# A fused two-block model on one core: narrower outputs in one mixer, a woven order in another

## The chip, the core and the metric

One core of a Trainium2 chip runs one program. The time is that of one launch on the device, in microseconds (us); the median of three runs is compared. TensorE (PE) multiplies, VectorE (DVE) and ScalarE (ACT) do elementwise work, GpSimd (POOL) and SyncE (SP) issue most DMAs here.

## What is computed

Two transformer blocks in a row on 256 tokens of width 1024, all in f32, two layers each. Block one puts 16 meta tokens ahead of the input and drops them at the end:

```python
for l in range(DEPTH):
    h = h + 0.5 * rmsnorm(swiglu(rmsnorm(h, g_pre_ffn1[l]), w_ffn1_gu[l], w_ffn1_down[l]), g_post_ffn1[l])
    mix = token_mixer(rmsnorm(h, g_pre_mix[l]), ...)      # causal softmax attention (fox) + gated linear attention (gla)
    h = h + rmsnorm(mix, g_post_mix[l])
    h = h + 0.5 * rmsnorm(swiglu(rmsnorm(h, g_pre_ffn2[l]), w_ffn2_gu[l], w_ffn2_down[l]), g_post_ffn2[l])
return h[:, BLOCK:]                                       # the 256 tokens
# in token_mixer
o_gla = from_heads(o_gla) * jax.nn.silu(gr)
y = jax.nn.sigmoid(g_merge_a) * (from_heads(o_fox) @ w_fox_o) + jax.nn.sigmoid(g_merge_b) * (o_gla @ w_gla_o)
return y @ w_out
```

Block two has a mLSTM mixer in its first layer and a dilated attention mixer in its second, which is the last mixer of the program:

```python
p = h @ w_q
q_d = rms_norm(p[..., :DIL_WIDTH]..., q_gain)             # 12 heads in 3 groups, 4 memory heads
# per group: s = q k^T * scale + bias(bucket of distance), masked, softmax, weighted by the groups' denominators
h_m = memory_cross_attention(p[..., DIL_WIDTH:], mem_n, w_mem_kv, mq_gain, mk_gain)   # 256 memory tokens, 4 heads
return jnp.concatenate([h_d, h_m], axis=-1) @ w_out
```

## The kernel before

One program holds a list of instructions for each engine, written out by hand, in an order that `weave` (L215) makes: a main generator yields once a step, and after each step every side generator goes on by one. Side work starts where it compares `c.step` with a number. Engines are tied by semaphores only.

**Weights.** All weights come as 723 slabs of up to 512 KB (128 partitions x 1024 f32) in the order in which `weights` (L140) lists them, through a ring of `RING = 7` slots (L26). SyncE issues slab u when `used` says that u − 7 is done (L430). ScalarE rounds a slab to fp32r (`whi`, L1243), VectorE takes the rest (`wlo`, L1906), both some `LEAD = 4` slabs ahead, and TensorE makes three products of eight matmuls each, high·high, high·low, low·high (`products`, L518). Activations are in such pairs too (`xhi`, `xlo`), with tokens as columns: 272 (`cols1`: 16 meta tokens and 256) or 256 (`cols2`).

**Order.** For each of two layers: ffn, `mixer1`, ffn. Then ffn 4, `mixer2a`, ffn 5, `shared_kv`, ffn 6, `mixer2b`, ffn 7. Each ffn has 22 steps j with a gate and an up slab, then 22 down slabs.

**`mixer1(L)`** (TensorE L711, ScalarE L1402, VectorE L2119). All projections have 272 columns in both layers. Softmax attention is done in 24 units a layer (`fox_units`, L415): 4 pairs of heads, query tiles of 128, 128 and 16 tokens, 2 heads, with 1, 2 and 3 key tiles. They are a side generator from step `FOX_AT = 13`, three deep: scores of unit i, turns of unit i − 2, values of unit i − 3. After the last step come the products with `w_fox_o` and `w_gla_o` (`fo`, `go`, L843), each half slab four k deep, gating on VectorE (L2357), and `wo`, which in the second layer already has 256 columns.

**`mixer2b`** (TensorE L1107, ScalarE L1812, VectorE L2652). (1) Four query slabs, the statistics matmul (`stat`), then the table of position biases: VectorE makes a 33x128 operand per head (`bias_table`, L2644), TensorE multiplies it with the one-hot table `ohb` (33x512), so that all 128 rows are equal, ScalarE copies it and sends 256 KB to `scratch` in DRAM (`bias_rows`, L1802); GpSimd reads it back shifted by one element a row (L505). (2) Eight query slabs in the order `B_ORDER`, each normed per head by `headnorms` (TensorE L617, ScalarE L1364, VectorE L2091): square, mean matmul in bank 7, Ln and Exp, four operations on VectorE, one slab at a time. (3) From step 4, eight dilated units (4 heads x 2 query tiles): scores of three groups, bias add and maximum, exp, division on VectorE (L2686), turns (L1163), copy, values; two deep, with turns that wait for the division. (4) The memory's keys and values (`mem_kv`, L891), whose operand pair `b_mp` is made there. (5) Eight memory units (`mem_attention`, L864), not woven with anything. (6) Eight output slabs (`bo`) in banks 4 to 7, `add_out` (L2592), and the filling of ffn 7's operands.

```python
sc = [bank[2][:, 0:W], bank[2][:, T:T + W], bank[3][:, 0:W]]
E.wait_ge(S("hn_out"), hn0 + (3, 6)[pair])
if n > 0:
    E.wait_ge(S("b_sb"), n)
if n >= 2:
    E.wait_ge(S("b_c"), n - 1)
```

## Time and profile before

| | us |
|---|---|
| median of three runs | 2567.19 (2565.28 to 2571.98) |
| profiled run | 2574.36 |
| its span | 2573.0 |
| TensorE busy | 2448.4 (95%) |
| VectorE, ScalarE busy | 1676.7 (65%), 1246.6 (48%) |
| last mixer, from `stat` to the end of `bo` | 2196.5 to 2373.6 |
| first block's second mixer, with `fo`, `go` | 930 to 1135.6 |

The granted TensorE clock of the profiled run is 0.967 of full on the mean. Busy time of TensorE includes slow matmuls, so it says nothing of the clock; the windows show both. The trace books an f32 matmul as two records and a transpose or an fp32r matmul as one; their ends are modelled, so that the distance between starts is the better price of a matmul in a dense stretch.

### The profile page before, as it was taken

The numbers are of one execution on the slowest core, as the hardware profiler recorded it, in microseconds if no ns is written. First come the engines' busy times: TensorE is split into PE (matmuls) and PEld (weight loads), VectorE is DVE, ScalarE is ACT, GpSimd is POOL, SyncE is SP. The second block draws the span as 40 slices with busy tenths as digits, with TensorE's granted clock in tenths as the row PEclk, the third lists the DMA queues.
The fourth block names the chain that finished last, engine by engine and source line by source line (L and its number), as shares of the span: only waits on it lengthen the run. The fifth ranks groups of instructions, "written<-read, shape, count | busy, mean of one in ns | idle before, by whom it ended". The sixth has DMA issues, their size and how long they took to land.

```text
span 2573.0 us, 45875 instructions
## 1 busy us (share of the span) xinstructions
PE 2448.4 (95%) x18769; PEld 2322.9 (90%) x18769; DVE 1676.7 (65%) x3006; ACT 1246.6 (48%) x2099; POOL 33.6 (1%) x63
## 2 busy tenths in 40 slices
PE   7999999999999989999999998999999999769999
PEld 6999788899999977899999998989998999457999
DVE  5656777776575487778648846756656765455664
ACT  5444455554354445556445634645445644334542
POOL 2000000000000000000000000000000000000000
PEclk9999999999999999999999998989999999677999
DMA  7655433565465453346655653427655665412653
GB/s 193 174 179 141 117 91 109 141 182 176 148 178 175 158 132 99 99 137 189 189 183 162 183 176 102 119 58 191 185 184 157 180 189 171 127 41 83 180 181 140
DMA packets 589729, 385.85 MB, mean 150 GB/s; under 512 B 44587, under 2 KB 564111, under 8 KB 589392
## 3 DMA queue, kind: packets, MB, share of 16 engines
q1 hardware_dynamic: 585408, 374.00, 50.5%
q10 hardware_dynamic: 2336, 5.92, 0.6%
q0 software_dynamic: 1776, 2.98, 0.4%
q8 instruction: 150, 2.46, 0.4%
q14 instruction: 59, 0.48, 0.1%
HBM read 378.59 MB, written 4.19 MB: 149 GB/s over the span
## 4 chain that ended last, share of the span: by engine, by line
PE 87%; DVE 8%; ACT 2%; issue 1%; DMA 1%; ACTq 0%; DVEq 0%
PE bank L516 86%; DVE wlo L1906 2%; DVE ry L1925 1%; DVE ry L1923 1%; PE bank L825 0%; ACT whi L1243 0%; DVE smh L2357 0%; DVE rst L1927 0%; PE bank L601 0%; ACT rst L1264 0%; DMA xs<-in_x 0%; PE bank L1163 0%; ACT rst L1266 0%; DMA wraw<-in_w_ffn_gu 0%; DVE ssb L2677 0%
## 5 line engine op out<-in xcount | busy, mean ns | idle before, releaser
L1906 DVE TENSOR_TENSOR wlo<-wraw,whi 128x1024 fp32r<-128x1024 f32 (+2 forms) x723 | 866.7, 1205 | 290.7 <-ACT whi L1243 287.3
L1243 ACT ACTIVATE whi<-wraw 128x1024 fp32r<-128x1024 f32 (+2 forms) x723 | 746.9, 1042 | 596.5 <-DMA wraw<-in_w_ffn_gu 175.2
L516 PE MATMUL bank<-xhi,whi 128*128 128x256 f32 (+2 forms) x4024 | 606.6, 291 | 40.7 <-ACT xhi L1279 24.6
L516 PE MATMUL bank<-xhi,wlo 128*128 128x256 f32 (+2 forms) x4024 | 592.8, 287 | 11.4 <-DVE wlo L1906 11.4
L516 PEld LDWEIGHTS bank<-xhi,whi 128*128 128x128 f32 (+1 forms) x4024 | 535.4, 190 | 63.0 <-ACT xhi L1279 27.1
L516 PE MATMUL bank<-xlo,whi 128*128 128x256 f32 (+2 forms) x4024 | 581.4, 285 | 0.0
L516 PEld LDWEIGHTS bank<-xhi,wlo 128*128 128x128 f32 (+1 forms) x4024 | 535.5, 190 | 15.4 <-DVE wlo L1906 15.1
L516 PEld LDWEIGHTS bank<-xlo,whi 128*128 128x128 f32 (+1 forms) x4024 | 528.2, 188 | 0.2
L516 PE MATMUL bank<-act_hi,wlo 128*128 128x256 f32 (+1 forms) x1408 | 400.5, 284 | 0.0
L516 PE MATMUL bank<-act_lo,whi 128*128 128x256 f32 (+1 forms) x1408 | 400.1, 284 | 0.0
L516 PE MATMUL bank<-act_hi,whi 128*128 128x256 f32 (+1 forms) x1408 | 399.1, 283 | 0.0
L516 PEld LDWEIGHTS bank<-act_hi,whi 128*128 128x128 f32 x1408 | 266.1, 189 | 0.0
L516 PEld LDWEIGHTS bank<-act_lo,whi 128*128 128x128 f32 x1408 | 264.8, 188 | 0.0
L516 PEld LDWEIGHTS bank<-act_hi,wlo 128*128 128x128 f32 x1408 | 264.3, 188 | 0.0
L1988 DVE TENSOR_TENSOR su<-bank,rst 128x256 f32<-128x256 f32 (+1 forms) x176 | 75.4, 429 | 224.0 <-PE bank L516 224.0
L1355 ACT ACTIVATE act_hi<-su 128x256 fp32r<-128x256 f32 (+1 forms) x176 | 73.6, 418 | 67.9 <-DVE su L1993 66.0
L1279 ACT ACTIVATE xhi<-hT,gain 128x256 fp32r<-128x256 f32 (+1 forms) x104 | 52.4, 513 | 98.0 <-DVE hT L1959 53.5
L1351 ACT ACTIVATE sg<-sg 128x256 f32<-128x256 f32 (+1 forms) x176 | 72.6, 412 | 47.2 <-DVE sg L1988 47.0
L1997 DVE TENSOR_TENSOR act_lo<-su,act_hi 128x256 fp32r<-128x256 f32 (+1 forms) x176 | 74.9, 426 | 7.8 <-ACT act_hi L1355 7.8
L1988 DVE TENSOR_TENSOR sg<-bank,rst 128x256 f32<-128x256 f32 (+1 forms) x176 | 74.7, 425 | 7.9 <-PE bank L516 7.7
L1993 DVE TENSOR_TENSOR su<-su,sg 128x256 f32<-128x256 f32 (+1 forms) x176 | 74.9, 426 | 2.0 <-DVE su L1988 0.5
L1918 DVE TENSOR_TENSOR ssum<-ssum,sqb 128x256 f32<-128x256 f32 (+1 forms) x120 | 51.7, 431 | 12.4 <-ACT sqb L1259 5.4
(396 smaller groups left out, 1815.9 us busy)
## 6 DMA issues: line engine op xcount, KB each, us to landing
wraw<-in_w_ffn_gu SPq DMA_DIRECT2D x176, 512.0 KB, 3.9
wraw<-in_w_ffn_down SPq DMA_DIRECT2D x88, 512.0 KB, 3.2
wraw<-in_ffn_w_gate SPq DMA_DIRECT2D x88, 512.0 KB, 3.9
wraw<-in_ffn_w_up SPq DMA_DIRECT2D x88, 512.0 KB, 3.9
wraw<-in_ffn_w_down SPq DMA_DIRECT2D x88, 512.0 KB, 3.3
wraw<-in_w_in SPq DMA_DIRECT2D x80, 512.0 KB, 3.9
wraw<-in_a_w_in SPq DMA_DIRECT2D x24, 384.0 KB, 3.2
wraw<-in_w_out SPq DMA_DIRECT2D x16, 512.0 KB, 3.8
```

The source lines that it names most:

```text
L516: return E.matmul(out_, lhsT, rhs, start=first, stop=last, skip_group_check=True)
L1243: A.activation(flat(whi, u), flat(wraw, u), ACT.Copy).then_inc(S("hi"), 1)
L1279: A.activation(xh[:, k, cols[0]:cols[1]], hT[:, k, cols[0]:cols[1]], ACT.Copy, scale=fill_gain(name)(k)).then_inc(S("xhi"), 1)
L1351: A.activation(s_g[:, j % 2, 0:n], s_g[:, j % 2, 0:n], ACT.Silu).then_inc(S("silu"), 1)
L1355: A.activation(a_hi[:, j, 0:n], s_u[:, j % 2, 0:n], ACT.Copy).then_inc(S("act_hi"), 1)
L1906: V.tensor_tensor(flat(wlo, u), flat(wraw, u), flat(whi, u).bitcast(F32), ALU.subtract).then_inc(lo_ready[u % RING], 1)
L1918: V.tensor_tensor(ssum[:, 0:n], ssum[:, 0:n], sqb[:, k % 2, 0:n], ALU.add).then_inc(S("ssum"), 1)
L1923: own(V.scalar_tensor_tensor(u, src, eps, dst, ALU.add, ALU.mult))
L1925: own(V.scalar_tensor_tensor(u, u, -0.5, dst, ALU.mult, ALU.mult))
L1988: V.tensor_tensor((s_g, s_u)[z][:, j % 2, 0:n], bank[b][:, 0:n], rst[:, cols[0]:cols[1]], ALU.mult).then_inc(S("gu_free"), 1)
L1993: V.tensor_tensor(s_u[:, j % 2, 0:n], s_u[:, j % 2, 0:n], s_g[:, j % 2, 0:n], ALU.mult).then_inc(S("act_mul"), 1)
L1997: V.tensor_tensor(a_lo[:, j, 0:n], s_u[:, j % 2, 0:n], a_hi[:, j, 0:n].bitcast(F32), ALU.subtract).then_inc(S("act_lo"), 1)
```

## The change

Two parts.

First, in the first block's second mixer (L = 1) queries, gates `gr`, `ma`, `mb` (24 of the slabs), `fo`, `go` and all between them have 256 columns, and the softmax units are 16: query tiles from token 16 and 144, with two and three key tiles.

```diff
-    FOX_N = 24
+        tiles = (TOK_TILES1, QUERY_TILES)[L]
+        return [(pair, i, t0, n, 2 * pair + hh, hh, t0 + n) for pair in range(4) for i, (t0, n) in enumerate(tiles) for hh in range(2)]
+
+    QUERY_TILES = [(N_META, P), (N_META + P, P)]
+    FOX_UNITS = [fox_units(L) for L in range(DEPTH)]
+    FOX_FROM = [0, len(FOX_UNITS[0])]
+    out_cols1 = [cols1, cols2]
+
+    def key_tiles(W):
+        return [(s0, min(n, W - s0)) for s0, n in TOK_TILES1 if s0 < W]
...
-                    project((name, L, s), x)
+                    project((name, L, s), xq if name == "fq" else x)
...
-                    project(("ma", L, s), x)
+                    project(("ma", L, s), xq)
...
-                        m = products(bank[b][:, 0:T1], u, slab_cols(u, q * P, P), lambda k, part: o[part][:, k, :], n_k=4)
+                        m = products(bank[b][:, 0:q1 - q0], u, slab_cols(u, q * P, P), lambda k, part: o[part][:, k, q0:q1], n_k=4)
```

Second, the last mixer has a new order. The bias rows go to ffn 6: the one-hot table is loaded after ffn 5, three matmuls give 4x512 rows each, ScalarE copies them into `ohb`, and GpSimd's queue sends each row 128 times to `scratch`. The pair `b_mp` is made in ffn 6 at j = 12 to 19. In the mixer, memory slabs are interleaved with query slabs, ten norms are a side generator of their own in banks 6 and 7, dilated units start at step 4 and are three deep, memory units start at step 10 and are woven with them, the division is folded into the turn (a matmul with a diagonal of 1/sum that ScalarE makes), and four output slabs run their first six k before the memory output is there. Each output slab has a bank of its own.

```diff
+B_HEAD = [("bq", 0, s) for s in (0, 2, 4, 1)]
+B_ORDER = [("bq", 0, 3), ("bq", 0, 5), ("mkv", 1, 0), ("bq", 0, 6), ("mkv", 1, 1), ("bq", 0, 7), ("mkv", 1, 2), ("mkv", 1, 3)]
+B_NORM_AT, B_NORM_STEP = (2, 2, 3, 3, 4, 5, 6, 7, 8, 9), (2, 3, 3, 4, 4, 5, 6, 7, 8, 9)
+B_UNIT_STEP, B_MEM_STEP, B_TURN_STEP = 4, 10, 11
+B_IDLE, B_EARLY = 5, 4
+B_ROW_AT = (4, 6, 8)
...
-        u = AT["d", 6, NF - 1]
+        u = AT["d", 5, NF - 1]
         G.wait_ge(S("used"), u + 1)
         G.dma_start(ohb[0:BUCKETS + 1, :], IN["onehot"]).then_inc(S("onehot"), 16)
+        for g in range(3):
+            G.wait_ge(S("b_row_c"), g + 1)
+            for q in range(4):
+                G.dma_start(IN["scratch"][4 * g + q:4 * g + q + 1], ohb[q:q + 1, 512 * g:512 * g + 512].unsqueeze(1).broadcast_to([1, P, 512])).then_inc(S("bias_out"), 16)
...
+                if F == 6 and j in B_ROW_AT:
+                    g = B_ROW_AT.index(j)
+                    if g == 0:
+                        E.wait_ge(S("onehot"), 16)
+                        E.wait_ge(S("par2"), 48)
+                    else:
+                        E.wait_ge(S("b_row_c"), g)
+                    mm(bank[6][0:4, :], tab[0:BUCKETS + 1, 4 * g:4 * g + 4], ohb[0:BUCKETS + 1, 512 * g:512 * g + 512], True, True).then_inc(S("b_row"), 1)
...
+                head_projects(B_HEAD, x, FILL["b"])
+                stat(cols2, 7)
+                yield
+                for i, key in enumerate(B_ORDER, HEAD):
+                    if key[0] == "mkv":
+                        E.wait_ge(S("mp_lo"), 2 * KD)
+                    if i >= HEAD + 2:
+                        E.wait_ge(S("evac"), c.proj - 1)
+                    c.proj += 1
+                    products(b_bank(i)[:, 0:T], AT[key], slab_cols(AT[key], 0, P), xm if key[0] == "mkv" else x).then_inc(S("used"), 1)
+                    yield
+                for _ in range(B_IDLE):
+                    yield
+                E.wait_ge(S("b_out"), 6)
+                for d in range(B_EARLY):
+                    u = AT["bo", 0, d]
+                    products(bank[d][:, 0:T], u, slab_cols(u, 0, P), xo, n_k=6, last=False)
+                    yield
...
+                    E.wait_ge(S("hn_sq"), hn0 + n + 1)
+                    if n >= 2:
+                        E.wait_ge(S("hn_out"), hn0 + (n - 1 if n < 4 else n))
+                    mm(b_norm_bank(n), C("mean64"), bsq[:, n % 6, :], True, True).then_inc(S("hn_ms"), 1)
...
+                    if 0 <= n - 2 < B_UNITS_N:
+                        h, i, rows, t0, W = b_unit(n - 2)
+                        E.wait_ge(S("b_d"), n - 1)
+                        for q in range(3 * (i + 1)):
+                            o = bank[2][:, q * P:q * P + P] if q < 4 else bank[6][:, (q - 4) * P:(q - 3) * P]
+                            m = mm(o, PPb[(n - 2) % 3][:, q * P:q * P + P], dgb[(n - 2) % 2], True, True)
+                        m.then_inc(S("b_t"), 1)
...
+                        A.activation(dgb[z], ident, ACT.Copy, scale=stat_a[:, 4 * z + 3:4 * z + 4]).then_inc(S("b_d"), 1)
...
-            if F == 5:
-                wait_h(E, H_OF_FILL["f5"], HEAD - 1)
+            if F in (5, 7):
+                wait_h(E, H_OF_FILL[f"f{F}"], HEAD - 1)
```

The tiles of the last mixer are laid out anew: those that ffn 6 fills (`bias`, `ohb`, `b_mp`) lie behind its own buffers.

## Rows read from the trace of the kernel before

**Rows 1.** The page's part 4, the chain that ended last by engine.
```profile
PE 87%; DVE 8%; ACT 2%; issue 1%; DMA 1%; ACTq 0%; DVEq 0%
```

**Rows 2.** Windows of the last mixer: us; busy by engine; clock, DMA share, GB/s.
```profile
2196.50:2219.40 22.90, 20.05 (x30) 7.06 (x28) 4.56 (x16) 7.49 (x14) 0.00 (x0) 0.64 0.67 211
2219.40:2290.80 71.40, 44.41 (x205) 36.08 (x205) 38.95 (x90) 25.90 (x55) 6.42 (x12) 0.69 0.20 58
2290.80:2325.00 34.20, 26.05 (x169) 22.57 (x169) 19.61 (x43) 14.80 (x33) 0.00 (x0) 0.84 0.16 47
2325.00:2348.50 23.50, 19.82 (x65) 10.83 (x64) 9.42 (x35) 8.49 (x29) 0.00 (x0) 0.59 0.08 22
2348.50:2373.60 25.10, 25.04 (x192) 25.04 (x193) 14.41 (x22) 11.19 (x15) 0.00 (x0) 0.91 0.49 142
```

**Rows 3.** Windows of the first block's second mixer, two of its stretches.
```profile
1050.00:1105.00 55.00, 55.00 (x403) 47.25 (x402) 41.28 (x103) 28.25 (x73) 0.00 (x0) 1.00 0.34 99
...
1111.60:1135.60 24.00, 24.00 (x192) 24.00 (x193) 17.80 (x32) 16.15 (x31) 0.00 (x0) 1.00 0.53 159
```

**Rows 4.** Windows, a stretch of ffn 6.
```profile
2060.00:2120.00 60.00, 60.00 (x513) 60.00 (x512) 37.72 (x62) 26.46 (x41) 0.00 (x0) 1.00 0.63 190
```

**Rows 5.** TensorE's waits, 2196.5 to 2373.6: us, times, longest.
```profile
PE bank L1163 <- DVE ssb L2677: 18.0, 7, 3.1
PE bank L516 <- DVE b_q L2115: 9.8, 3, 3.4
PE bank L516 <- DVE b_mp_lo L2394: 5.3, 1, 5.3
```

**Rows 6.** TensorE's timeline in the last mixer: start, us, line, out<-in, idle before.
```profile
2262.56 1.56 PE L516 MATMUL bank<-k_sh,b_q 64*128 64x256 f32 x6
2266.96 0.52 PE L1163 MATMUL bank<-cst,ppb 128*128 128x128 f32 x3 [2.84 <-DVE ssb L2677]
...
2273.38 0.59 PE L516 MATMUL bank<-sqb,cst 128*128 128x256 f32 x2
2273.90 0.93 PE L516 MATMUL bank<-k_sh,b_q 64*128 64x128 f32 x6
```

**Rows 7.** TensorE's groups by form, last mixer: count, busy us, mean ns, idle.
```profile
L516 PE MATMUL bank<-ohb,rst 33*128 33x512 f32 x24 | 19.0, 968 | 2.8 <-DVE rst L2648 2.8
```

**Rows 8.** TensorE's groups by form, 2296 to 2325.
```profile
L516 PE MATMUL bank<-ptb,v_sh 128*64 128x128 f32 x36 | 5.2, 296 | 0.0
```

**Rows 9.** Timeline at the start of the shared keys.
```profile
1968.65 1.18 PE L516 MATMUL bank<-xhi,whi 128*128 128x256 f32 x8 [1.33 <-ACT whi L1243]
```

**Rows 10.** VectorE's groups by form, last mixer.
```profile
L1906 DVE TENSOR_TENSOR wlo<-wraw,whi 128x1024 fp32r<-128x1024 f32 x18 | 21.9, 1218 | 0.0
...
L1923 DVE SCALAR_TENSOR_TENSOR ry<-bank,sqb 128x256 f32<-128x256 f32 x10 | 4.2, 425 | 16.4 <-ACT sqb L1266 16.4
...
L2680 DVE TENSOR_REDUCE stat_a<-ssb 128x1 f32<-128x768 f32 x4 | 3.8, 953 | 0.1
```

**Rows 11.** ScalarE's groups by form, last mixer.
```profile
L1243 ACT ACTIVATE whi<-wraw 128x1024 fp32r<-128x1024 f32 x19 | 19.9, 1052 | 0.3 <-DMA wraw<-in_b_w_out 0.2
...
L1264 ACT ACTIVATE sqb<-bank,eps 128x256 f32<-128x256 f32 x10 | 4.6, 462 | 2.6 <-PE bank L516 2.6
...
L1832 ACT ACTIVATE ppb<-ssb,stat_a 128x768 f32<-128x768 f32 x4 | 3.7, 936 | 16.4 <-DVE stat_a L2682 16.4
```

**Rows 12.** TensorE's groups by form, 930 to 1135.6: units of 16 queries.
```profile
L516 PE MATMUL bank<-ka,qa 128*16 128x272 f32 x16 | 5.1, 398 | 0.0
...
L516 PE MATMUL bank<-ybuf,fv 128*64 128x16 f32 x32 | 3.2, 214 | 0.0
```

**Rows 13.** Timeline, the first fo product.
```profile
1111.60 0.74 PE L516 MATMUL bank<-ofp_hi,whi 128*128 128x272 f32 x4 [1.01 <-DVE ofp_lo L1978]
```

**Rows 14.** All DMA issues: KB each, median us from issue to landing.
```profile
bias_scratch<-bias ACTq DMA_DIRECT2D x12, 256.0 KB, 2.0
```

**Rows 15.** DMA, 940.42 to 940.64: GB/s in 40 slices of 5.5 ns.
```profile
GB/s 0 0 0 0 0 0 0 198 0 0 0 0 0 0 198 1 0 0 0 0 0 0 199 0 0 0 0 0 0 1 198 0 0 0 0 0 0 1 0 0
```

More of the change, by code:

```diff
@@ L197, in weights @@
     ffn2(6, "ffn1", 1)
-    for s in B_ORDER:
-        cols(("bq", 0, s), IN["b_w_q_2"][0], s * P)
-    mem_kv(1)
+    for name, l, s in B_HEAD + B_ORDER:
+        cols((name, l, s), IN["b_w_q_2"][0] if name == "bq" else IN["w_mem_kv_2"][1], s * P)
     for d in range(KD):
@@ L615, in values @@
                 yield
-        def headnorms(keys, x, before=lambda: None):
-            for i in range(len(keys) + 1):
-                if i < len(keys):
-                    keys[i]()
-                if i > 0:
-                    E.wait_ge(S("hn_sq"), c.hn + 1)
-                    if c.hn > 0:
-                        E.wait_ge(S("hn_out"), c.hn)
-                    before()
-                    mm(bank[7][:, 0:T], C("mean64"), sqb[:, (i - 1) % 2, 0:T], True, True).then_inc(S("hn_ms"), 1)
-                    c.hn += 1
-                yield
         def turn_rows():
@@ L1123, in project_b @@
-            def project_b(i):
-                first_project(keys, i, x, FILL["b"])
-                if i == 0:
-                    bias_rows()
-            def main():
-                yield from headnorms([lambda i=i: project_b(i) for i in range(8)], x)
-                yield from mem_kv(1, b_mp, [ohb[:, 0:T], ohb[:, T:2 * T]], lambda: None)
-            outs = ((6, 0), (6, T), (5, 0))
-            def dilated():
-                units = [(h, i) for h in range(DIL_HEADS) for i in range(2)]
-                for n in range(len(units) + 2):
-                    if n < len(units):
-                        h, i = units[n]
-                        pair, rows = h // 2, slice(64 * (h % 2), 64 * (h % 2) + 64)
-                        while c.step < (4, 7)[pair]:
-                            yield
-                        t0, _ = TOK_TILES2[i]
-                        W = t0 + P
-                        sc = [bank[2][:, 0:W], bank[2][:, T:T + W], bank[3][:, 0:W]]
-                        E.wait_ge(S("hn_out"), hn0 + (3, 6)[pair])
+            xm = lambda k, part: b_mp[part][:, k, :]
@@ new lines, in norms, with turns @@
+            def norms():
+                for n in range(len(B_NORMS)):
+                    while c.step < B_NORM_AT[n]:
+                        yield
+                    E.wait_ge(S("hn_sq"), hn0 + n + 1)
+                    if n >= 2:
+                        E.wait_ge(S("hn_out"), hn0 + (n - 1 if n < 4 else n))
+                    mm(b_norm_bank(n), C("mean64"), bsq[:, n % 6, :], True, True).then_inc(S("hn_ms"), 1)
+                    c.hn += 1
+            def turns():
+                for s in range(2):
+                    while c.step < B_TURN_STEP + s:
+                        yield
+                    E.wait_ge(S("evac"), c.first + 10 + s + 1)
+                    E.wait_ge(S("hn_out"), hn0 + len(B_NORMS))
+                    E.wait_ge(S("tv_c"), c.tv)
+                    turn_values([b_vz[:, 0, :], b_vz[:, 1, :]], s, TOK_TILES2, 7)
@@ L1146, in dilated @@
+            def dilated():
+                for n in range(B_UNITS_N + 3):
+                    while c.step < B_UNIT_STEP + n:
+                        yield
+                    if n < B_UNITS_N:
+                        h, i, rows, t0, W = b_unit(n)
+                        E.wait_ge(S("hn_out"), hn0 + (3, 6)[h // 2])
                         if n > 0:
                             E.wait_ge(S("b_sb"), n)
-                        if n >= 2:
-                            E.wait_ge(S("b_c"), n - 1)
@@ L1183, in mixer2b @@
+            weave(main(), [norms(), turns(), dilated(), memory()], c)
             E.wait_ge(S("mem_o"), 4)
-            E.wait_ge(S("evac"), c.proj)
             for d in range(KD):
                 u = AT["bo", 0, d]
-                if d >= 4:
-                    wait_h(E, H_OF_FILL["f7"], d - 4)
-                products(bank[4 + d % 4][:, 0:T], u, slab_cols(u, 0, P),
-                         lambda k, part: hd[part][:, k, :] if k < 6 else b_hm[part][:, k - 6, :]).then_inc(S("used"), 1)
+                if d < B_EARLY:
+                    products(bank[d][:, 0:T], u, slab_cols(u, 0, P), xo, n_k=2, first=False, k0=6).then_inc(S("used"), 1)
+                else:
+                    products(bank[d][:, 0:T], u, slab_cols(u, 0, P), xo).then_inc(S("used"), 1)
@@ L1402, in mixer1 @@
         def mixer1(L):
+            q0, q1 = out_cols1[L]
             def main():
@@ L1858, in mixer2b @@
+            weave(main(), [norms(), turns(), dilated(), memory()], c)
+            c.proj += 12
             for d in range(KD):
@@ L2697, in mixer2b @@
+            weave(main(), [norms(), dilated(), memory()], c)
             for d in range(KD):
                 ahead(("bo", 0, d))
-                add_out(d, ("bo", 0, d), "f7", 4 + d % 4)
+                add_out(d, ("bo", 0, d), "f7")
             fill_low("f7", cols2, KD - 1)
```

659 lines of the change are left out of this document (326 added, 333 removed).

## The prediction

> **What bounds the kernel now.** I read the page first: TensorE holds 87% of the chain of work that ended last [rows 1], so over most of the program only fewer TensorE instructions, or a faster clock, shorten the time. The 40 slices of the page name one exception, so the second view is the table of windows over the last mixer, from the statistics matmul at 2196.5 us to the end of its output projection at 2373.6 us [rows 2]. There TensorE is busy 135.4 of 177.1 us, and at a granted clock between 0.59 and 0.91, against 1.00 in both windows of the first block's second mixer [rows 3] and in the ffn before it [rows 4]. The third view, TensorE's waits in that stretch, says where the idle time is: 18.0 us in seven waits for the added bias scores (`ssb`), 9.8 us for normed queries (`b_q`), 5.3 us for the low half of the memory operand [rows 5]. The timeline shows the same as a rhythm: scores at 2262.56, then 2.84 us of nothing before the turns at 2266.96 [rows 6]. Elsewhere (second mixer, ffn 6) TensorE never idles: there the question is only how many columns and instructions go [rows 3, 4].
>
> The profiled execution took 2574.36 us with a span of 2573.0; the median of three is 2567.19. Sums are made against 2574.4, and 7.2 us come off at the end.
>
> **Part A, the last mixer.** How much work it is at full clock: busy time by granted clock in the five windows is 12.8 + 30.6 + 21.9 + 11.7 + 22.8 = 99.8 us [rows 2]. The 12 bias rows leave this stretch: the group of 24 records took 19.0 us, so one 512-column matmul (two records) took 1.58 us at a mean clock of 0.64; at full clock that is 0.79 (half) to 1.01 (by the mean), I take 0.86, together 10.3 us [rows 7]. That leaves 89.5. Counting up instead: eight products (24 matmuls of 0.1175 us, from 60.00 us for 513 [rows 4]) 22.6; ten norms at 0.52 (from 2273.38 to 2273.90) 5.2; four pairs of dilated units, short and long, each with scores of 0.93 + 1.56, less 0.1 of overlap, and 18 records of value matmuls at 0.125 (the row's mean is 0.144 with part of it at a lower clock) and as many for the turns: 6.9, so 27.6 [rows 6, 8]; memory units 11.7 by the fourth window, 2 more by the turns; output projection 22.8; statistics and value turns 1.5. Sum 94.
>
> The new turns are what makes this more than 89.5. They multiply by a diagonal matrix, an f32 matmul that the trace books as two records, in place of a transpose of one record. No row shows this form here. Nearest rows: a transpose, 0.52 us for three [rows 6], and a value matmul, 0.25 for its two records [rows 8]. With 52 of them (36 and 16) the cost is 0 to +6 us. I take +5, as the form is that of the value matmul.
>
> What is not work. (1) From statistics to the fourth product after it: the norms of the first four slabs wait for the activation engine, as in the shared keys, where one such wait was 1.33 us [rows 9]. Four products 11.3, five norms 2.6, first scores 0.9, statistics 0.7, waits 8.8, an estimate from the one row (the first norm's chain about two of 1.33, two waits behind queued copies of 1.33, two later norms at 1.75): 24.3, and half of it at the lower clock, as in the first window of before, adds 4.5: 29. (2) Five steps with a unit, a norm and a product each. TensorE needs 4.8 to 7.2 us for one, but ScalarE and VectorE hand each other a loop in program order: exp of a unit 0.87 (0.94 for a long one, less for a short one), high copy 1.05, square 0.45, Ln and Exp 0.95, the four operations of a norm 1.87, additions and maximum 2.1 (long unit's maximum 0.95), hops 0.4: 7.7 us [rows 10, 11]. 5 × 7.7 = 38.5. In before this step took about 11 us (2262.56 to 2273.90 [rows 6]) since the turns, too, waited in it. (3) Five steps without product or with the last units: 23.5 (units 5 × 4.2, turns, first memory units). (4) Wait for the last `b_out` 1.0. (5) Four early output slabs, six of eight k each, beside memory units: 4 × 2.16 + four memory units at 1.64 = 15.2. (6) Two empty steps and the last high and low halves 3.5. (7) The rest of the output projection 22.8 - 8.6 = 14.2, and the new wait for four `h` tiles at the head of ffn 7: 1.5; behind it queue only ffn 7's first products. Sum 126.4. So −50.7.
>
> Bounds. Best: 92 of work (the turns at a transpose's price), 10 of start and 6 of end, 108: −69. Worst: the loop keeps 10 us a step (+11.5), and the low clock stays through (3) to (5), +12: 150: −27.
>
> The Trainium skill (TensorE: Matmul & The Clock Gate, HAM oscillation) says that idle gaps between bursts of matmuls bring the engine back to its slow clock. The fourth window agrees in kind: 0.59 with 3.7 us of its 23.5 idle [rows 2]. By this rule the removed waits would pay twice, which is the best end above.
>
> **Part B, the bias rows, in ffn 6.** Three matmuls of 33x512 at 0.86: +2.6 us on TensorE, which is busy 60.00 of 60 there [rows 4, 7]. The two orders on TensorE (`b_row_c` of the group before) wait on something 11 us old: 0. Three copies of 4 partitions, eight high and eight low copies of `b_mp` on ScalarE and VectorE (8 × 0.5 each) go beside 26.46 and 37.72 us busy of 60: 0, cover 22 us on VectorE; without it 4 us. Removed from the mixer with them: 12 copies and 12 DMA issues on ScalarE's queue, `rst` tables on VectorE, the 5.3 us wait [rows 5]; all within part A.
> On POOL's queue the one-hot load, now behind ffn 5, then 12 broadcasts and 12 reads. Nothing else waits on that queue; what they do to the weight slabs is rival D.
>
> **Part C, the first block's second mixer.** TensorE is busy 55.00 of 55 and 24.00 of 24 at clock 1.00 [rows 3], so columns count in full. (1) 24 projections of 256 columns for 272: a matmul of 272 costs 24.00/192 = 0.125 us, one of 256 costs 0.117 [rows 3, 4]: 24 × 24 × 0.0075 = −4.3, of which I take −4.0, since the smaller matmuls between them stay. (2) `fo`/`go`: 192 × 0.0075 = −1.4. (3) Softmax units. Gone are the eight with 16 queries: scores 5.1 us, values 3.2 [rows 12], turns about 2.3: 10.6. Added: the remaining 16 get one more key tile of 16 rows, a turn and a value matmul of about 0.2 each, 16 × 0.39 = 6.2. Net −4.4. Bounds: 0 (small matmuls as dear as they look) and −8. (4) Before the first `fo` TensorE waits 1.01 us for the low half of the last softmax pair [rows 13], behind a unit's last small matmuls; with 16 units for 24 that pair is done eight steps earlier, and wait and matmuls go from this place: −1.5. Sum −11.3 (−6 to −14). What is late next: VectorE, at 41.28 of 55, has 14 us of room [rows 3], and slabs in the ring have a step less cover; 0.
>
> **Sum.** −50.7 + 2.6 − 11.3 = −59.4: profiled 2515.0, median 2508.
>
> **The rivals.**
> B, the loop or the clock doesn't give: the worst end of part A, −27 + 2.6 − 11.3 = −36: 2531. For it: every step still hands over four times between engines, and the norms still come one by one. Against: the turns now lag by one unit more.
> C, TensorE-bound: −69 + 2.6 − 11.3 = −78: 2489. For it: the work is only 92 to 94. Against: a loop of 7.7 us where TensorE needs 4.8 to 7.2.
> D, slower. Each new broadcast reads one 2 KB row of one partition 128 times, and there are 12, 3.15 MB in ffn 6, where the weight stream has TensorE saturated and DMA engines busy 0.63 [rows 4]. In before, 128 partitions gave their 256 KB in 2.0 us of landing [rows 14]. The only transfer of before out of one partition sends packets of 1.09 KB (198 GB/s in a slice of 5.5 ns) that come 42 ns apart [rows 15]: 26 GB/s. If that is what one partition gives, a broadcast takes 10 us, twelve 118 us. If an engine holding such a packet passes no weights, the ring of seven slabs leaves six of cover, 6 × 2.82 = 17 us, and some weights slip in between: +95 us, 2603. It decides the sign where the twelve hold the weights for over 59 + 17 = 76 us, 6.3 us each. Against: four packets in a row may as well be one DMA engine's own pace, so the row doesn't tell a partition's limit from an engine's; and other queues may pass. The table would still be ready by the mixer.
> The Trainium skill speaks for D: SBUF — State Buffer (Door 1: The DMA port swizzle) gives one port to partitions 0 to 3, about 27 GB/s, and DMA: Bandwidth & Descriptors (Back-pressure in remote DMA) says, of writes, that stalled ones stall their engine's other queues. By the two together the time would be D's.
> D/2, half of it (the weights lose 20 to 60 us beyond the ring): 2520 to 2570.
> E, little comes: C's part is bound by other engines and A's gain is lost to a new order of waits: 2560.
>
> **How the numbers follow.** Forecast as summed 0.52, B 0.14, C 0.10, D 0.16, D/2 0.05, E 0.03. Likeliest 2508. Its own range is 2495 to 2523. The range runs from just below C to above B and the cheaper half of D/2: 2487 to 2545; left out are D, the rest of D/2 and E, about 2 in 10. A measurement of this kernel tells about 0.3%, 7.7 us, from no change. D/2 splits 0.03 faster, 0.01 within, 0.01 slower, E 0.01 and 0.02. Faster by more: 0.52 + 0.14 + 0.10 + 0.03 + 0.01 = 0.80; within: 0.01 + 0.02 = 0.03; slower: 0.16 + 0.01 = 0.17.
>
> **What would show it.** Windows of the last mixer: 126 us, clock above 0.8 after the start; largest waits of TensorE no longer `ssb` but `hn_out` and `hn_sq` (queries, squares); steps of 7.7 us. ffn 6: three matmuls of 33x512 inside a full TensorE, no wait for `whi` or `wlo`; with D instead, long waits there for `whi` and slabs landing in 10 us and more. Second mixer 11 us shorter with no new waits. Wrong would be: steps of 10 us or a clock of 0.7 (B), or ffn 6 longer than 20 us over before (D).

## The result and the profile after

The changed kernel takes 2593.91 us (median of 4 runs, 2590.11 to 2599.79), the kernel before in the same measurement 2569.59: a ratio of 1.0095 (95% interval 1.007 to 1.012), 24 us slower, where 2508 us was forecast. The profiled execution has a span of 2590.4 us for 2573.0.

The distances between the statistics matmuls, one at the start of each stage, say where the 17.4 us between the two spans are.

| stretch | before | after | difference | forecast |
|---|---|---|---|---|
| second mixer of block one, to the next statistics | 235.3 | 229.0 | -6.3 | -11.3 |
| ffn 6, from its statistics to those of the last mixer | 188.5 | 281.5 | +93.0 | +2.6 (rival D: +97.6) |
| last mixer, to the end of its output projection | 177.1 | 114.3 | -62.8 | -50.7 |
| all else | 1972.1 | 1965.6 | -6.5 | 0 |

The last row holds no edit but the wait for four `h` tiles at the head of ffn 7, which cost nothing (TensorE idles 1.9 us there in both). Most of the row (5.5 us) is block two's first mixer, 206.4 us in the profiled execution of before and 200.9 in that of after. Its granted clock was 0.80 in the first 33.4 us and 0.88 in the last 73.0 before, 0.85 in the first 33.5 and 0.92 in the last 67.4 after, and 1.00 between.

Part 4 and part 3 of the page of after: the chain by engine, then by line; the DMA queues with packets, MB and the time their packets took as a share of 16 engines.

```profile
q0 software_dynamic: 2736, 6.13, 4.5%
...
PE 83%; DVE 8%; DMA 3%; ACT 2%; SPq 2%; issue 1%; ACTq 0%; DVEq 0%
PE bank L564 82%; DVE wlo L1957 3%; DMA wraw<-in_ffn_w_up 3%; SPq L479 2%; ACT whi L1279 1%; DVE ry L1976 1%; DVE ry L1974 1%; PE bank L865 0%; DVE rst L1978 0%; DMA xs<-in_x 0%; ACT rst L1300 0%; DVE smh L2387 0%; PE bank L646 0%; ACT rst L1302 0%; ACT xhi L1315 0%
```

In before TensorE held 87% of the chain [rows 1]. Now 3% is a DMA of weights and 2% SyncE's queue. GpSimd's queue q0 moved 6.13 MB, 1.6% of the bytes, and its packets took 4.5% of the engines' time.

TensorE's waits of after from 1990 to 2277 us (waited for: us in total, times, longest):

```profile
PE bank L564 <- ACT whi L1279: 48.0, 4, 25.8
PE bank L564 <- ACT ohb L1379: 31.4, 1, 31.4
```

Windows of after over ffn 6 (us; busy PE, PEld, DVE, ACT, POOL with counts; granted clock, DMA share, GB/s), to be held against the one full window of before [rows 4]:

```profile
2022.00:2036.40 14.40, 14.37 (x115) 13.17 (x113) 4.46 (x8) 2.73 (x4) 1.58 (x4) 1.00 1.00 65
2036.40:2067.70 31.30, 0.00 (x0) 0.00 (x0) 2.34 (x3) 3.23 (x6) 0.00 (x0) 0.57 0.97 84
2067.70:2092.00 24.30, 24.26 (x170) 22.34 (x170) 6.71 (x12) 4.21 (x6) 2.06 (x4) 0.85 1.03 55
2092.00:2111.70 19.70, 0.00 (x1) 0.04 (x1) 0.12 (x1) 1.21 (x2) 0.00 (x0) 0.59 0.93 84
2111.70:2130.60 18.90, 16.81 (x120) 16.23 (x120) 9.60 (x16) 6.26 (x10) 2.07 (x4) 0.89 1.06 98
2130.60:2156.30 25.70, 0.00 (x0) 0.00 (x1) 0.09 (x1) 1.17 (x2) 2.58 (x5) 0.55 0.95 69
```

GpSimd's queue in the same time (start, us, line, count, idle before and what ended it), and the transfers (KB each, median us to landing):

```profile
2021.46 2.12 POOL L553 DMA_DIRECT2D bias_scratch<-ohb  x4 [84.06 <-ACT ohb L1379]
2067.97 2.06 POOL L553 DMA_DIRECT2D bias_scratch<-ohb  x4 [44.39 <-ACT ohb L1379]
2112.63 2.13 POOL L553 DMA_DIRECT2D bias_scratch<-ohb  x4 [42.60 <-ACT ohb L1379]
2153.72 6.36 POOL L557 DMA_DIRECT2D bias<-bias_scratch  x12 [38.97 <-DMA bias_scratch<-ohb]
```

```profile
bias_scratch<-ohb POOLq DMA_DIRECT2D x12, 256.0 KB, 26.4
```

Three bursts of four broadcasts start at 2021.5, 2068.0 and 2112.6. Behind each TensorE goes on for a while with the slabs that are there (the ring's cover: 14.9 us after the first, from 2021.5 to 2036.4) and then stands still: windows of 31.3, 19.7 and 25.7 us without work for it. In these three the DMA engines are 93 to 97% busy and move 69 to 84 GB/s, a third to a half of what ffn 6 draws [rows 4]. A broadcast lands 26.4 us after its issue (the median, with the time behind the others of its burst; the four land some 9 us apart), where the 256 KB out of 128 partitions took 2.0 [rows 14]. After each gap the clock is low for some us (0.85, 0.89). The idle time adds to 79 us; new matmuls and slow ones make the rest of the 93.

The last mixer of after in windows, in the order of the prediction's terms (1), (2), (3), (5) and (6) with (7):

```profile
2277.00:2305.40 28.40, 18.91 (x118) 16.28 (x117) 18.89 (x39) 13.29 (x25) 0.00 (x0) 0.88 0.48 130
2305.40:2338.00 32.60, 28.58 (x198) 24.24 (x197) 24.85 (x61) 17.93 (x39) 0.00 (x0) 1.00 0.29 82
2338.00:2358.00 20.00, 19.56 (x130) 15.04 (x130) 9.80 (x34) 12.55 (x39) 0.00 (x0) 1.00 0.00 1
2358.00:2372.90 14.90, 14.90 (x104) 12.60 (x104) 7.49 (x18) 8.15 (x21) 0.00 (x0) 1.00 0.00 1
2372.90:2391.30 18.40, 17.47 (x143) 16.66 (x142) 9.94 (x18) 9.19 (x15) 0.00 (x0) 1.00 0.75 192
```

The clock is 0.88 in the first of them and full in the rest, where it was between 0.59 and 0.91 [rows 2]. TensorE's waits there, and the new turns:

```profile
PE bank L564 <- DVE b_q L2691: 8.4, 4, 3.7
PE bank L564 <- DVE ssb L2710: 2.2, 2, 1.8
PE bank L564 <- DVE b_km L2691: 1.6, 1, 1.6
```

```profile
L564 PE MATMUL bank<-dgb,ppb 128*128 128x128 f32 x72 | 10.2, 286 | 0.0
L564 PE MATMUL bank<-ptb,v_sh 128*64 128x128 f32 x72 | 9.5, 278 | 0.4 <-DVE hd_lo L2029 0.4
```

The 18.0 us of waits for `ssb` [rows 5] are 2.2 us now, in two waits.

### The profile page after: what moved, and what is told of

It reads as the page before. It is cut to its first block, busy times and chain, and to the rows that moved or that the text cites. A ratio compares the mean times of both kernels' runs of the same rounds, so it can differ in the third digit from the quotient of the medians.

```text
span 2590.4 us, 45742 instructions
## 1 busy us (share of the span) xinstructions
PE 2412.1 (93%) x18763; PEld 2302.5 (89%) x18763; DVE 1652.2 (64%) x2938; ACT 1241.5 (48%) x2090; POOL 39.7 (2%) x75
## 3 DMA queue, kind: packets, MB, share of 16 engines
q0 software_dynamic: 2736, 6.13, 4.5%
## 4 chain that ended last, share of the span: by engine, by line
PE 83%; DVE 8%; DMA 3%; ACT 2%; SPq 2%; issue 1%; ACTq 0%; DVEq 0%
PE bank L564 82%; DVE wlo L1957 3%; DMA wraw<-in_ffn_w_up 3%; SPq L479 2%; ACT whi L1279 1%; DVE ry L1976 1%; DVE ry L1974 1%; PE bank L865 0%; DVE rst L1978 0%; DMA xs<-in_x 0%; ACT rst L1300 0%; DVE smh L2387 0%; PE bank L646 0%; ACT rst L1302 0%; ACT xhi L1315 0%
## 5 line engine op out<-in xcount | busy, mean ns | idle before, releaser
L564 PE MATMUL bank<-xhi,wlo 128*128 128x256 f32 (+2 forms) x4024 | 592.8, 287 | 11.3 <-DVE wlo L1957 11.3
L1988 DVE SCALAR_TENSOR_TENSOR xlo<-hT,gain,xhi 128x256 fp32r<-128x256 f32 (+1 forms) x104 | 50.0, 487 | 15.5 <-ACT xhi L1315 15.5
```

Of the source, the lines that this page charges most:

```text
L564: return E.matmul(out_, lhsT, rhs, start=first, stop=last, skip_group_check=True)
L1988: V.scalar_tensor_tensor(xl[:, k, cols[0]:cols[1]], hT[:, k, cols[0]:cols[1]], fill_gain(name)(k), xh[:, k, cols[0]:cols[1]].bitcast(F32), ...
```

## The experiments

My theory after the result: the broadcasts out of one partition take the time of the DMA engines, and the weights wait behind them; all the rest of the change does about what was forecast. Rivals: the work moved into ffn 6 is at fault and not the DMAs; GpSimd's queue or a broadcast as such is slow, wherever it reads; the new mixer is only short because the weights were ready early after the long ffn 6.

### Where the broadcasts read

For these the matmul of the one-hot table was made 128 rows wide, each head's row 32 times, so that the source of a broadcast is free to choose. VectorE spreads the table once in ffn 6; a matmul of 33x128 weights takes the place of one of 33x4.

```diff
+                if F == 6 and j == 1:
+                    V.wait_ge(S("par2"), 48)
+                    V.tensor_copy(tabw.rearrange("p (h r) -> p h r", r=32), tab[0:BUCKETS + 1, :].unsqueeze(2).broadcast_to([BUCKETS + 1, 12, 32])).then_inc(S("b_tab"), 1)
...
-                    mm(bank[6][0:4, :], tab[0:BUCKETS + 1, 4 * g:4 * g + 4], ...
+                    mm(bank[6][:, :], tabw[:, P * g:P * g + P], ...
...
-                    A.activation(ohb[0:4, 512 * g:512 * g + 512], bank[6][0:4, :], ACT.Copy) ...
+                    A.activation(ohb[:, 512 * g:512 * g + 512], bank[6][:, :], ACT.Copy) ...
```

**s1**, one partition 128 times, the four of a burst from partitions 0, 32, 64 and 96:

```diff
-                G.dma_start(IN["scratch"][4 * g + q:4 * g + q + 1], ohb[q:q + 1, ...].unsqueeze(1).broadcast_to([1, P, 512]))
+                G.dma_start(IN["scratch"][4 * g + q:4 * g + q + 1], ohb[32 * q:32 * q + 1, ...].unsqueeze(1).broadcast_to([1, P, 512]))
```

> The changed kernel, but the product of the one-hot table is 128 rows wide, so that head q's row stands in partitions 32q to 32q+31; each broadcast still reads one partition 128 times, the four of a burst now from partitions 0, 32, 64 and 96 in place of 0, 1, 2, 3. Theory (the reads of one partition, or of the few next to it, are served at about 26 GB/s, and a DMA engine that holds such a read passes no weights): if the four transfers of a burst run one after the other, a burst is as long as in the changed kernel, 35 to 40 us, and from the statistics of ffn 6 to those of the last mixer it takes 275 to 285 us (281.5 there, 188.5 before). If the four run side by side, 10 us a burst and 191 to 200. Rival (any broadcast of 2 KB packets from GpSimd's queue is slow): 281. Another rival (the long stretch comes from the extra work in ffn 6 and not from the DMAs): 281 here and in the three others.

**s4one**, four neighbouring partitions 32 times each:

```diff
+                G.dma_start(IN["scratch"][4 * g + q].rearrange("(a b) u -> a b u", b=32), ohb[32 * q:32 * q + 4, ...].unsqueeze(1).broadcast_to([4, 32, 512]))
```

> As s1, but each broadcast reads four neighbouring partitions (32q to 32q+3), 32 times each. Theory of a limit on a group of neighbouring partitions: as s1, bursts of 35 to 40 us, stretch 275 to 285 us. Rival, a limit on each partition by itself: four times as fast, bursts of 10 us, stretch 191 to 200.

**s4four**, four partitions that are four apart (`ohb[32 * q:32 * q + 16:4]`):

> As s1, but each broadcast reads four partitions that are four apart (32q, +4, +8, +12), 32 times each. Theory of a limit on groups of neighbours, and also of one on each partition: 10 us a burst, under the ring's cover of 14 to 17 us, stretch 191 to 200 us. Rival (GpSimd's queue or broadcasts as such): 275 to 285.

**s32**, 32 partitions four times each (`ohb[32 * q:32 * q + 32]`, `b=4`):

> As s1, but each broadcast reads 32 partitions, four times each. All instructions on the four engines are those of the changed kernel but for a wider product (128 columns of weights for 4) and one more copy on VectorE. Theory: a burst in 3 to 6 us, no wait for weights in ffn 6, stretch 190 to 193 us, the whole 90 us under the changed kernel: ratio to before 0.973 to 0.976 (2500 to 2508 us). Rival (a broadcast as such, or GpSimd's queue, holds the weights): no gain, ratio 1.00 to 1.01. Rival (gain of the new mixer is partly due to the weights that were ready early after the long ffn 6): ratio 0.978 to 0.985.

**s4off**, as s4one, but head q's four neighbours begin at partition 36q (`ohb[36 * q:36 * q + 4]`):

> As s4one (each broadcast reads four neighbouring partitions, 32 times each, with four DMA engines, the four broadcasts of a burst side by side), but head q's rows are read from partitions 36q to 36q+3 in place of 32q to 32q+3. Theory A: partitions 0 to 3 and 32 to 35 share one way out of 27 GB/s, 64 to 67 and 96 to 99 another, so in s4one the four transfers had two ways, 55 GB/s and 22 us a burst; here they have four, and a burst takes 10 to 12 us, under the ring's cover: stretch of ffn 6 192 to 200 us, the whole near 2505 to 2515. Theory B: each group of four neighbours gives some 12 to 14 GB/s more by itself, wherever it is: 22 us a burst as in s4one, stretch 234 us, the whole 2548.

Measured, with the stretch of ffn 6 from statistics to statistics. The last burst is from the issue of its first transfer to the landing of its last; "landing" is the median of the twelve from issue to landing. Of the experiments in this table all but s32 were run once:

| run | a burst reads | last burst, us | landing, us | ffn 6, us | time, us |
|---|---|---|---|---|---|
| changed kernel | partitions 0, 1, 2, 3, one after the other | 41.1 | 26.4 | 281.5 | 2593.9 (four runs) |
| s1 | partitions 0, 32, 64, 96, one after the other | 39.1 | 25.3 | 271.4 | 2588.0 |
| s4one | four groups of four at 0, 32, 64, 96 | 24.8 | 21.6 | 234.0 | 2548.6 |
| s4off | four groups of four at 0, 36, 72, 108 | 16.9 | 12.5 | 201.1 | 2522.1 |
| s4four | 16 single partitions, four apart | 11.3 | 7.6 | 192.4 | 2511.0 |
| s32 | 32 partitions each | 7.8 | 5.3 | 193.0 | 2514.7 (2499.0 to 2515.5) |

s32 against before: ratio 0.9781 (0.9757 to 0.9805), where 0.973 to 0.976 was expected; its stretch of 193.0 us is as expected, its burst of 7.8 us longer than the 3 to 6. The ratio lies in the range of the rival of early weights, which p2fix takes up. The bursts are read off GpSimd's timeline, here the last rows of s4one and of s4off:

```profile
2082.87 2.69 POOL L554 DMA_DIRECT2D bias_scratch<-ohb  x4 [27.78 <-ACT ohb L1380]
2107.62 6.44 POOL L558 DMA_DIRECT2D bias<-bias_scratch  x12 [22.07 <-DMA bias_scratch<-ohb]
```

```profile
2068.83 2.70 POOL L554 DMA_DIRECT2D bias_scratch<-ohb  x4 [16.08 <-ACT ohb L1380]
2085.73 6.46 POOL L558 DMA_DIRECT2D bias<-bias_scratch  x12 [14.20 <-DMA bias_scratch<-ohb]
```

and the landings off the list of DMA issues, here of s4off (KB each, median us to landing):

```profile
bias_scratch<-ohb POOLq DMA_DIRECT2D x12, 256.0 KB, 12.5
```

The DMA view of the middle of a burst has the packets, MB and busy share by queue, q0 the broadcasts and q1 the weights. Of the changed kernel from 2030 to 2055 us (25 us), of s4one from 2028 to 2042 (14 us), of s4off from 2033 to 2041 (8 us), of s32 from 2020 to 2024 (4 us):

```profile
q0 software_dynamic: 212, 0.67, 94.7%
q1 hardware_dynamic: 83, 0.04, 0.6%
```

```profile
q0 software_dynamic: 181, 0.74, 95.1%
```

```profile
q0 software_dynamic: 207, 0.77, 95.9%
```

```profile
q0 software_dynamic: 304, 1.00, 82.3%
q1 hardware_dynamic: 458, 0.23, 19.4%
```

s1 to s32 do the same work in ffn 6 (the changed kernel the same but for its narrower product of the table), and all six issue twelve transfers of 256 KB from GpSimd's queue, so the work, the queue and the broadcast as such are ruled out as the cause. What is left is where the transfer reads, and how its pattern is cut: one partition 128 times, four 32 times, 32 four times. The three s4 runs have one pattern and differ in place alone. In the middle of a burst the broadcasts get 0.67 MB in 25 us, 27 GB/s, in the changed kernel, and there the weights pass 0.04 MB, next to nothing: the DMA engines are held, 95% of their time by q0. s4one has 0.74 MB in 14 us, 53 GB/s, s4off 0.77 in 8 us, 96 GB/s, s32 1.00 in 4 us, 250 GB/s, and beside it the weights go on at 57.

s1 is nearly as slow as the changed kernel (271.4 us for the expected 275 to 285): its four transfers go in the main one after the other, and each of them has one partition. In s4one and s4off the four go side by side: the last three of a burst land together, in s4one 21 to 25 us after their issue. (The first is booked after 3 to 5 us, but all four count on one semaphore, so that this count doesn't say which had landed.) The two differ only in where the groups lie, and s4off has nearly twice the rate. So a group of four neighbours has one way out of about 27 GB/s, and partitions 0 to 3 share it with 32 to 35: one way in the changed kernel, two (53) in s4one, four (96) in s4off. That is theory A. Theory B, which gave s4off a burst of 22 us and a stretch of 234, is ruled out by it, and a limit on each partition by itself by s4one. The Trainium skill (SBUF — State Buffer, Door 1: The DMA port swizzle) gives this map, one port for partitions 0 to 3 and 32 to 35 and another for 36 to 39, at about 27 GB/s; these runs agree with the map, and with the rate at 27 GB/s for one port, 53 for two and 96 for four.

s4off missed the numbers of theory A: a burst of 16.9 us for 10 to 12, a stretch of 201.1 for 192 to 200, 2522.1 us for 2505 to 2515. TensorE lost 5.6 us there to one wait for the row copy; the length of the burst, 62 GB/s over all of it where the middle has 96, stays open. s4one's 234.0 us lies between its two expectations: the first took the four transfers to go one after the other, and they went over two ways at once.

**spread**, the changed kernel with its one-partition broadcasts, one after every fourth slab:

```diff
+                G.wait_ge(S("used"), AT["g", 6, 6] + 4 * (4 * g + q) + 1)
                 G.dma_start(IN["scratch"][4 * g + q:4 * g + q + 1], ohb[q:q + 1, ...
```

> The changed kernel with its broadcasts from one partition, but not in three bursts of four: one after every fourth slab, so that each hold of 9.8 us lies within the ring's cover of 14 us. Theory (a DMA engine that holds a broadcast packet is lost for the weights, so what counts is the sum of time of the DMA engines): 12 broadcasts at 9.4 us and 60 slabs at 1.8 us are 220 us in a stretch in which TensorE needs 155 and has 14 us of cover: 40 to 60 us more than without, stretch 230 to 250 us, the whole 2545 to 2565. Rival (only what is longer than the cover is lost): stretch 191 to 195, the whole near 2505.

2542.1 us in one run, and 221.0 us for the stretch: 28 us over s32's 193.0, and 60 under the changed kernel. TensorE's waits of spread from 1990 to 2250:

```profile
PE bank L565 <- ACT whi L1280: 12.1, 7, 3.8
PE bank L565 <- DVE wlo L1958: 7.1, 3, 4.0
```

The rival (nothing lost, since each hold is under the cover) is out. A broadcast by itself lands 11.5 us after its issue, the median of the twelve of this run. How I read it: the ring is not full again when the next hold begins; no run shows its level. The theory's size was off too, 28 us for 40 to 60, 221.0 us for 230 to 250 and 2542.1 for 2545 to 2565. It charged 1.8 us of the DMA engines for a slab, from their busy share in ffn 6 [rows 4]; a likely reason, not shown, is that this share counts time in which packets are only held. What a slab takes of the engines was not measured.

### The two parts apart

**p1**, the first part of the change alone on the kernel before (`mixer1` and `fox_units` of the changed kernel, the rest untouched):

> The kernel before with the first part of the change alone: second layer's queries, gates and outputs for 256 columns, 16 softmax units. Forecast of the prediction: 11.3 us less (ratio 0.9956). From the trace of the changed kernel the theory is now that TensorE's work falls by about 10 us but two waits of ScalarE and VectorE come out from under it (2.1 us for the low half of the linear attention's last output, and 2 us more at the head of the output projection): 6 to 8 us less, ratio 0.9970 to 0.9978; from the statistics of this mixer (924) to those of the next ffn 229 us, 235.3 in the kernel before. Rival (all of it is hidden or lost): 1.000.

Ratio 0.9979 (0.9965 to 0.9993), 2564.0 against 2568.3 us; the mixer takes 228.9 us, as expected (229), and the ratio is at the upper end of what was expected (0.9970 to 0.9978). Two half edits, each run once, say what belongs to what.

**p1cols**, columns alone:

```diff
-    QUERY_TILES = [(N_META, P), (N_META + P, P)]
+    QUERY_TILES = TOK_TILES1
```

> The kernel before with the narrower columns alone: 24 projections and fo and go for 256 columns, but still 24 softmax units on the tiles of before (the scores of the 16 meta queries use queries left from the layer before, and nothing reads their rows). By the prediction's terms the mixer is 4.0 + 1.4 = 5.4 us shorter, 229.9 from statistics to statistics. Theory of exposed waits: TensorE still has the units' work to cover the last output of the linear attention, so fo starts with the 1.0 us wait of before, and only the head of the output projection gives back up to 2 us: 230 to 232.

**p1units**, units alone (both edits are against p1; the output projection keeps its 256 columns):

```diff
-    out_cols1 = [cols1, cols2]
+    out_cols1 = [cols1, cols1]
...
-            out_cols = out_cols1[L]
+            out_cols = cols1 if L == 0 else cols2
```

> The kernel before with the units alone: 16 softmax units, but 272 columns everywhere (the 16 first columns of the attention output are those left from the layer before, and are dropped). By the prediction's terms 4.4 + 1.5 = 5.9 us less: 229.4. Theory of exposed waits: the wait for the linear attention's last low half, not there in the kernel before, takes 1.5 to 2.5 us back: 231 to 232.5.

The mixer takes 230.7 us with the columns alone (-4.6, forecast -5.4) and 231.8 with the units alone (-3.5, forecast -5.9); together -6.4, less than the sum of 8.1. TensorE's waits from 900 to 1160 us show the exposed one, of p1cols, then of p1units, then of p1:

```profile
PE bank L523 <- DVE ofp_lo L1988: 1.0, 1, 1.0
```

```profile
PE bank L523 <- DVE ogp_lo L1988: 2.0, 1, 2.0
```

```profile
PE bank L523 <- DVE ogp_lo L1988: 2.1, 1, 2.1
PE bank L523 <- DVE wlo L1916: 1.0, 2, 0.7
```

With 24 units TensorE is late enough at the first `fo` to wait only for the softmax output, 1.0 us, as in before [rows 13]. With 16 it comes earlier and waits 2.0 for the low half of the linear attention's last output, `ogp_lo`, which no edit of this change made earlier. Behind it, the head of the output projection waits 1.0 us for `wlo` in place of 0.7, at a clock of 0.87 in p1 (1126.8 to 1140 us) where it was 1.00 in before (1135.6 to 1148).

**p2fix**, s32 without the first part:

> The kernel s32 (broadcasts from 32 partitions) without the first part of the change, so with the new last mixer and the bias rows in ffn 6 alone. Theory: 62.9 us less in the last mixer, 2.6 to 4 more in ffn 6, so 59 us under the kernel before, ratio 0.976 to 0.978. By the prediction's sum (50.7 less and 2.6 more) 48 us, 0.9813. Rival (the gain in the last mixer is a gift of weights that came early): 30 to 40 us, 0.985 to 0.988.

Ratio 0.9797 (0.9779 to 0.9815), some 52 us less, between the theory's 59 and the 48 of the prediction's sum; the last mixer takes 117.0 us and ffn 6 193.8. In this kernel, as in s32 (114.2 us), ffn 6 loses nothing to the broadcasts, so the rival of a gift by early weights, which gave 30 to 40 us, is out. Of the 7 us that it falls short of the expectation 3 are in the mixer and 1 to 3 in ffn 6 (5.3 over before, where 2.6 to 4 were expected); the rest lies outside the edited stages. The 3 us in the mixer are a slower start of the same code, seen again below.

### The last mixer

**slack**, s32 with one more copy of 256 columns on ScalarE in each of the last five norms:

```diff
+                    if n >= 5:
+                        A.activation(spare[:, 0:T], b_norm_bank(n), ACT.Copy)
                     rsqrt(bsq[:, n % 6, :], b_norm_bank(n), "hn_rsq")
```

> The kernel s32 with one more copy of 256 columns on ScalarE (0.4 us) ahead of Ln and Exp in each of the last five norms, to nobody's use. In the prediction's term for the five steps ScalarE and VectorE hand each other a loop of 7.7 us that bounds the step: then the copies cost 5 x 0.45 = 2.2 us, and the last mixer takes 116.5 us for 114.3. Theory now (TensorE bounds most of these steps, at 6.5 us, and waits only 4 us in all five): 0 to 1 us, 114 to 115.3.

The mixer takes 118.4 us in the one run, more than either side expected. The windows say where. Of s32, then of slack, the same four pieces of work:

```profile
2183.70:2207.60 23.90, 14.45 (x86) 12.26 (x85) 16.31 (x31) 12.40 (x23) 0.00 (x0) 0.86 0.52 143
2207.60:2212.50 4.90, 4.89 (x34) 4.15 (x34) 3.05 (x10) 0.89 (x2) 0.00 (x0) 1.00 0.18 55
2212.50:2244.60 32.10, 28.06 (x196) 24.03 (x195) 24.39 (x60) 17.95 (x39) 0.00 (x0) 1.00 0.29 83
2244.60:2297.90 53.30, 51.93 (x373) 44.30 (x374) 27.30 (x68) 29.82 (x75) 0.00 (x0) 1.00 0.26 67
```

```profile
2196.90:2222.00 25.10, 15.65 (x86) 13.45 (x85) 16.31 (x31) 12.41 (x23) 0.00 (x0) 0.80 0.50 138
2222.00:2230.00 8.00, 7.99 (x34) 7.11 (x34) 4.52 (x11) 2.55 (x5) 0.00 (x0) 0.57 0.09 28
2230.00:2262.00 32.00, 29.32 (x195) 25.14 (x194) 22.95 (x58) 17.71 (x41) 0.00 (x0) 0.95 0.29 83
2262.00:2315.30 53.30, 51.90 (x373) 44.30 (x374) 27.26 (x68) 29.76 (x75) 0.00 (x0) 1.00 0.26 67
```

All five copies lie in the third window (from 2230.5 to 2257.8 us, 0.36 us each), and it takes 32 us in both. But the two don't come to it alike. In slack the pieces before it ran at a clock of 0.80 and 0.57 for 0.86 and 1.00, and while TensorE was slow there ScalarE and VectorE got ahead: 5 and 11 instructions in the second window for 2 and 10. A fairer measure is a run with the same mixer, no copies, and the same start. s4four has it, its first three windows:

```profile
2193.20:2218.30 25.10, 15.69 (x86) 13.47 (x84) 16.31 (x31) 12.41 (x23) 0.00 (x0) 0.80 0.48 135
2218.30:2226.30 8.00, 7.94 (x34) 7.13 (x34) 4.53 (x11) 2.55 (x5) 0.00 (x0) 0.57 0.13 38
2226.30:2256.90 30.60, 27.79 (x195) 23.93 (x194) 22.90 (x58) 16.31 (x36) 0.00 (x0) 1.00 0.31 87
```

The first two are those of slack, the third is 30.6 us for 32.0, and its whole mixer takes 117.0. So do those of spread and p2fix, with the same start and 30.6 and 30.7 us. So 2.8 of the 4.2 us over s32 are the start, which is slow in runs without copies too, and 1.4 us come from copies of 1.8 us in all. That is between the two expectations (2.2, and 0 to 1): in these steps ScalarE has little room, and most of what is added to it comes through. The clock of 0.57 stands behind the waits of the first window; why the same code starts slowly in one run and not in another no run tells.

**best**, s32 with the third and fourth norm's mean matmul in banks of their own:

```diff
-        return bank[6 if n in (1, 3) else 7][:, 0:T]
+        return bank[{1: 6, 2: 2, 3: 3}.get(n, 7)][:, 0:T]
...
-                    if n >= 2:
-                        E.wait_ge(S("hn_out"), hn0 + (n - 1 if n < 4 else n))
+                    if n >= 4:
+                        E.wait_ge(S("hn_out"), hn0 + (1 if n == 4 else n))
```

> The kernel s32 with the mean matmuls of the third and fourth norm in banks 2 and 3, which are free by then, in place of banks 6 and 7: they no longer wait for the norms before them, and the fifth waits for the first alone. In s32, as in the changed kernel, TensorE idles 3.7, 2.1 and 2.4 us there. Theory (these waits set the start of the last mixer, and bring the low clock): the first two waits go, with some of the low clock behind them: 4 to 8 us less in the last mixer, 106 to 110 us, and 0.2 to 0.3% less than s32, ratio to before 0.975 to 0.977. Rival (ScalarE and VectorE are the bound there, TensorE only waits for them a little later): 0 to 2 us, 0.978.

The last mixer takes 110.0 us, at the edge of the theory's 106 to 110, and TensorE's waits for `b_q` fell from 8.3 to 4.5 us. The time is 2501.8 us, ratio 0.9733 (0.972 to 0.9746), 71 us under the kernel before, and better than the 0.975 to 0.977 expected:

```profile
PE bank L565 <- DVE b_q L2695: 4.5, 2, 4.3
```

It beats s32 (0.9757 to 0.9805) and both kernels of the case. Of the 13 us between the medians of s32 and best the mixer accounts for 4 to 7, by s32's quick start or the slow one; the rest lies outside the edit.

## Why the prediction was wrong

**The step that failed** is in part B: the sum charged the twelve broadcasts nothing for what they do to the weight slabs (+2.6 us for the whole part) and left that to rival D, at a chance of 0.16. Measured, they hold the DMA engines so long that TensorE stands still 79 us for want of slabs, and the stretch is 93.0 us longer. Rival D itself had the mechanism, the place and nearly the price: 95 us, and 97.6 for the stretch with the 2.6. What failed is its weight. It was set so low on the argument that packets 42 ns apart could be one DMA engine's own pace [rows 15], so that the row told nothing of a partition's limit. That was true of the row. But nothing in the trace spoke for the other reading either. The Trainium skill (SBUF — State Buffer, Door 1: The DMA port swizzle) gives about 27 GB/s for one port, and the row shows 26. With a chance of a half the range would have had to reach to 2603. The likeliest case was wrong with it.

**Part B.** The copies of `b_mp` and of the rows were hidden, as said. "The two orders on TensorE wait on something 11 us old: 0" failed: the third bias matmul waited 31.4 us for the row copy, which stood on ScalarE's queue behind the rounding of a slab that had not landed. It's the same lack of slabs, seen from another engine. D's cover was 14.9 us where six slabs at 2.82 gave 17: the ring was not full of landed slabs. When the burst began TensorE had the slab in work and four behind it, the last of which landed some 4 us later. ScalarE rounded that at 2025.61 us and then waited for the next landing, here in its timeline:

```profile
2064.01 1.06 ACT L1279 ACTIVATE whi<-wraw 128x1024 fp32r<-128x1024 f32 x1 [37.03 <-DMA wraw<-in_ffn_w_gate]
```

In the runs that lose nothing to the broadcasts ffn 6 takes 192.3 to 193.8 us, 3.8 to 5.3 over before and 2 to 4 over p1 (190.1), for the forecast +2.6.

**Part A** went further than forecast, 114.3 for 126.4 us. Term by term: start 28.4 (29); five steps 32.6 (38.5); steps without product 20.0 (23.5) and no wait for `b_out` (1.0); early slabs 14.9 (15.2); the rest 18.4 (3.5 + 14.2 + 1.5, the wait for `h` was nothing). The term mis-sized most is the loop of 7.7 us. Measured steps are 6.5 us, with TensorE busy 28.6 of 32.6. That ScalarE is on the path there was right, since 1.4 of the 1.8 us that slack adds come through; the length was not. The sum added all pieces in a row, and some of them must overlap; which, no run shows. With the slow start the same mixer takes 117.0 us, still 9 under the forecast. The bounds, 108 to 150, held. The new turns cost 10.2 us for 72 records, 0.142 each, the price of a value matmul (0.132), as taken. The clock rose as forecast: 0.88 in the start, with TensorE idle 9.5 of 28.4 us, and 1.00 in the five steps, with 4.0 of 32.6 idle.

**Part C** gave 6.3 for 11.3. Columns -4.6 for -5.4; units -3.5 for -5.9. Term (4), -1.5 at the first `fo`, had the wrong sign: a wait of 1.0 went and one of 2.1 came, on the other side's output. I had named what is late next as VectorE's room over the whole stretch, 14 us, where the question was which single result the first `fo` needs last. The 1 to 2 us at the head of the output projection and of the ffn behind it weren't in the sum at all.

**The sum** without D comes near by luck in part: s32 is forecast plus 7 (2514.7 for 2508; by ratio 0.978 for 0.977), with A 9 to 12 better than forecast, and C 5 and B 2 worse. What is left, some 9 to 12 us, is in no term. The five runs of s32 differ by 16 us, the longer ones at the lower mean clock (2499.0 at 0.986, 2515.5 at 0.977).

## What to carry to other kernels

Ask of each DMA how many partitions it reads, not only how many bytes: a broadcast out of one partition is cheap to issue and moves 27 GB/s while it takes 95% of the DMA engines' time. So replicate on chip first, here by a matmul with repeated weight columns (the three matmuls with 33x128 weights take TensorE 3.4 us in s32, those with 33x4 3.9 in the changed kernel), and send from many partitions that lie well apart or from 32 neighbours: both lost nothing here. A transfer that nobody waits for still has a price where a weight stream has TensorE full, and spreading it out within the ring's cover lessens the loss but doesn't end it. A rival that the profile can't exclude, with a price above the whole gain, weighs more than 0.16.
